# Block kernel with S5, block attention, retention and expert layer: decay rates on ScalarE, parameters loaded first, four blocks rounded by GpSimd, part of the second angles on ScalarE, key gains in tables and in a copy

## The chip, the cores and the metric

The kernel runs on one core of a Trainium2 chip. The metric is the device time of one execution in microseconds (us); lower is better. Three runs of the kernel before took 913.27, 913.45 and 913.71 us.

## The reference

One layer of a model with 256 tokens of width 1024 is computed. Its input projection feeds three mixers side by side; their outputs go through a second projection, and a layer of 16,384 experts follows.

```python
h = rms_norm(x, norm1_g)
ua, qb, kb, vb, qc, kc, vc, gc = split(h @ w_in)         # 256, 3 x 512, 4 x 256 columns
# S5 mixer on ua: 16 groups x 64 complex states
dt = exp(log_dt); mag = exp(lam_re * dt)                 # decay rates
ar = mag * cos(lam_im * dt); ai = mag * sin(lam_im * dt)
fr = ((ar - 1) * lr + ai * li) / (lr*lr + li*li); fi = (ai * lr - (ar - 1) * li) / (lr*lr + li*li)
bb = f * b; state[t] = a * state[t-1] + bb @ ua[t]; y = real(c @ state) + ua * d
ya = y' * sigmoid(y' @ w_glu), y' = gelu(y)
# block attention: rms_unit(q) * gq and rms_unit(k) * gk, the first 16 of 64 dims rotated; softmax
# retention: q, k rotated; decayed scores
y = concat(rms_unit(ya), rms_unit(yb), yc) * mix_out_g
x = x + y @ w_out
x = x + peer_layer(rms_norm(x, norm2_g))                 # 8 heads, top 16 of 128 x 128 experts
```

## The kernel before

**Products in halves.** A 32-bit operand is split into a high part, rounded to the format that TensorE multiplies at full rate, and a low part, the rest. Each product is three matmuls: high by high, high by low, low by high (lines 438 to 440). The projection weights (`w_in`, `w_out`, `w_q`) are cut into slices of 128 rows by 512 columns, numbered m = 0, 1, 2, ... in the order of use; slices 0 to 39 are `w_in`. A slice passes a line of four engines: a DMA on SyncE brings a group of eight slices (2 MB) into one of three places of `w_ring`; ScalarE rounds the slice into `w_hi` (`slices_high`, line 1387); GpSimd subtracts into `w_lo` (`slices_low`, line 1728); TensorE multiplies both token tiles, six matmuls of 512 columns (`by_slices`). `w_hi` and `w_lo` have four places each, so ScalarE may round slice m only once TensorE is done with slice m-4 (semaphore `half_used`). The order of every engine is written out by hand.

**The start.** x is transposed (line 415) and scaled by the norm gain into eight blocks `hT[:, k]`: blocks 0 to 3 by ScalarE (`full`, line 1426), 4 to 7 by VectorE (line 882). The first 256 columns of `w_in`, which give `ua`, are multiplied unsplit (line 455). ScalarE rounds the eight blocks into `h_hi` (`rounded`, line 1433) and GpSimd subtracts into `h_lo` (line 1759); slice k needs both. GpSimd alternates: blocks 0 to 3, slice 0, block 4, slice 1, and so on. Ahead of all this it computes `mag`, the exponential of `expo`, with a polynomial of small dependent instructions (lines 1736 to 1748).

**The S5 mixer in pieces.** VectorE derives `dt`, `expo` and the angles from the parameters `vec`, then the input matrices `bb`. The phases of the scan are a table of cosines and sines (`pc`, `pS`) in two halves of four tiles: `phase_turns` (VectorE, three passes of 1024 columns: product with time, add a rounding constant, take the fraction) then `phase_sines`, `phase_sizes`, `phase_cosines` (ScalarE). The drive of the states is multiplied in four parts by `drive(n)` on TensorE (line 430) between slices, and each part is scanned by `states(n)` on VectorE (lines 817 and 996). `drive(0)` stands after slice 2, `drive(1)` after slice 12. `states(0)` uses PSUM banks 6 and 7.

**Attention.** VectorE rotates queries (tables with the query gain in them) and keys. Each key tile is first multiplied by the gain (line 817, two instructions of 512 columns). TensorE transposes them (line 491) and ScalarE copies them out of PSUM (`heads_back`, line 1451). The negated output matrix `c_neg` (line 1081), in the place of `b_s`, is made by VectorE between `states(2)` and `states(3)`. The semaphore `consts_in` counts five loads (rotation table, `s5_c`, `w_glu`, `mask`, `decay`), 16 for each; VectorE first waits for all 80 behind `states(0)`.

**The rest.** From about 120 us on the second projection and the experts run in loops which the change leaves alone.

Of the kernel before, what the change touches and what calls it, by code (L numbers as in the profile page):

```python
# [57 lines left out]
POOL_HIGH = (34, 36)  # L58
TAIL = FRONT + 4 * KC
# [34 lines left out]
V_N = V_GQK + 2 * HD  # L94
# [28 lines left out]
def build(nc, x, w_in, vecs, consts, rots, decay, mask, s5_b, s5_c, w_glu, w_out, w_q, keys, u_t, v, out, spill):  # L123
    with ExitStack() as ctx:
# [84 lines left out]
        mask_s = rawf[:, 0:S]  # L209
        rope_q = rawf[:, 320:384].rearrange("p (f t d) -> p f t d", f=2, t=TT)  # L210
# [33 lines left out]
        turn_ready, phase_ready = sem("phase_turns_ready"), sem("phases_ready")  # L244
        bb_ready, bT_psum, bT_ready = sem("bb_ready"), sem("bT_in_psum"), sem("bT_ready")
# [18 lines left out]
        th_ready, tl_ready = sem("transposed_high_ready"), sem("transposed_low_ready")  # L264
        pq_ready, sc_psum, sc_ready = sem("pq_ready"), sem("keys_scores_in_psum"), sem("keys_scores_ready")
# [39 lines left out]
        phi_p = ps[:, 5, 0:8]  # L305
# [4 lines left out]
        spare = tiny(1)  # L310
        mag_k, mag_rest, mag_power = tiny(8), tiny(8), tiny(8)
# [96 lines left out]
        def _(pe):  # L408
# [51 lines left out]
            def by_slices(n, ks):  # L460

                for k in ks:
                    m = KC * (n - 1) + k
                    if n == 1:
                        pe.wait_ge(th_ready, k + 1)
# [183 lines left out]
            def out_slices(n, places):  # L649

                for i in places:
                    k = MIX_ORDER[i]
                    if n == 0:
                        pe.wait_ge(th_ready, KC + i + 1)
# [33 lines left out]
            for n in range(2):  # L688
                for k in range(KC):
                    if n == 0:  # L690
                        pe.wait_ge(th_ready, 2 * KC + k + 1)
# [29 lines left out]
            def keys_turn(t, groups=None, first=False, first_group=False, wide=()):  # L721

                for s in range(UN):
# [4 lines left out]
                    for h in range(2):  # L728
                        if first and s == 0:
                            pe.wait_ge(th_ready, 3 * KC + 4 * h + 4)  # L730
                            pe.wait_ge(tl_ready, 3 * KC + 4 * h + 4)
# [76 lines left out]
        def _(dve):  # L808
# [18 lines left out]
            V.memset(eps_4, 4 * EPS).then_inc(zeros_ready, 1)  # L827

            def transposed_low(gain, n, order=range(KC), banks=range(4), first=0):

                for i, k in enumerate(order, first):
                    dve.wait_ge(th_ready, n * KC + 2 * (i // 2) + 2)
# [23 lines left out]
            for part in (RC1, RC2, RC3):  # L856
# [13 lines left out]
            did(tt(cols(V_GQK + HD + ROPE, HD - ROPE), cols(V_GQK + HD + ROPE, HD - ROPE), cols(V_GQK + ROPE, HD - ROPE),  # L870
                   ALU.mult))
# [59 lines left out]
            tt(bb[:, 1], bb[:, 1], t_b, ALU.add).then_inc(bb_ready, 1)  # L931
            dve.wait_ge(bT_psum, 1)
            dve.wait_ge(u_ready, 1)
            did(V.tensor_copy(phi_p, phi))
# [89 lines left out]

            states(0)
            phase_turns(1, 6, phi_p)
# [18 lines left out]
            step(rotate([k_p[t][:, :, 0:ROPE] for t in range(TT)], k_p, half_rope, rope[:, 0], rope[:, 1], scratch(ROPE),  # L1045
# [35 lines left out]
            V.tensor_scalar(c_neg, c_s, -1.0, None, ALU.mult).then_inc(c_ready, 1)  # L1081
            dve.wait_ge(c_ready, 1)
# [96 lines left out]
            for k in range(KC + 2):  # L1179
                if k >= 2:  # L1180
                    dve.wait_ge(th_ready, 3 * KC + k - 1)
# [185 lines left out]
        def _(act):  # L1367
# [37 lines left out]

            def phase_sines(c):
# [22 lines left out]
            def rounded(ks):  # L1429

                for k in ks:
                    act.wait_ge(full_act if k < 4 else full_dve, k % 4 + 1)
# [16 lines left out]
            def heads_back(a, d_):  # L1449
                act.wait_ge(rotT_psum, a + 1)  # L1450
                A.activation(d_, ps[:, 6:8, :].rearrange("p b (h t) -> p (b h) t", h=2), ACT.Copy).then_inc(rotT_ready, 1)
# [15 lines left out]
            act.dma_start(vec[:], vecs).then_inc(params_in, 16)  # L1467
            act.dma_start(ident, consts[:, C_ID:C_ID + P]).then_inc(con_in, 16)
            act.dma_start(rawf[:, 256:256 + ROPE_N], rots[:, 0:ROPE_N]).then_inc(rope_in, 16)
            act.wait_ge(zeros_ready, 4)  # L1470
            A.activation(spare, quarter, ACT.Sqrt)
            squares_x(0)
            squares_x(1)
            act.wait_ge(params_in, 16)
            for k in range(4):
                full(k)
            act.wait_ge(sumsq_x, TT)
            root(ss_x, 0, 1.0 / D)
            rounded(range(0, 4))
# [4 lines left out]
            slices_high(range(0, 1))  # L1484
            rounded(range(4, KC))
# [3 lines left out]
            for t in range(TT):  # L1489
                A.activation(u_tok[:, t, :], ps[:, 4 + 3 * t, 0:S5_CH], ACT.Copy,  # L1490
                             scale=rx[:, t:t + 1]).then_inc(u_tok_ready, 1)
            slices_high(range(2, 3))
            act.wait_ge(uT_psum, 1)
            A.activation(uT, ps[:, 5, :].rearrange("p (c t) -> p c t", c=S5_C), ACT.Copy).then_inc(u_ready, 1)
            phase_sines(0)
            slices_high(range(3, 4))
            phase_sizes(0)
            slices_high(range(4, 5))
            phase_cosines(0)
            slices_high(range(5, 11))  # L1500
# [10 lines left out]
            heads_back(0, mqT)  # L1511
# [7 lines left out]
            heads_back(1, mkT)  # L1519
# [196 lines left out]
        def _(pool):  # L1716
# [14 lines left out]
            def step(ins):  # L1731
                did(ins)
                settle()

            pool.wait_ge(expo_ready, 1)
            step(G.tensor_scalar(mag_k, expo, float(1 / np.log(2)), ROUND, ALU.mult, ALU.add))
            step(G.tensor_scalar(mag_k, mag_k, -ROUND, None, ALU.add))
            step(G.tensor_scalar(mag_rest, mag_k, -LN2_1, None, ALU.mult))
            step(G.tensor_tensor(mag_rest, mag_rest, expo, ALU.add))
            step(G.tensor_scalar(mag_power, mag_k, -LN2_2, None, ALU.mult))  # L1740
            step(G.tensor_tensor(mag_rest, mag_rest, mag_power, ALU.add))
            step(G.tensor_scalar(mag_k, mag_k, -127.0, 127.0, ALU.max, ALU.min))
            step(G.tensor_scalar(mag_power.bitcast(mybir.dt.int32), mag_k, 127.0, float(2 ** 23), ALU.add, ALU.mult))
            step(G.tensor_scalar(mag, mag_rest, EXP_C[0], EXP_C[1], ALU.mult, ALU.add))
            for c_ in EXP_C[2:] + [1.0]:
                step(G.tensor_tensor(mag, mag, mag_rest, ALU.mult))
                step(G.tensor_scalar(mag, mag, c_, None, ALU.add))
            G.tensor_tensor(mag, mag, mag_power, ALU.mult).then_inc(mag_ready, 1)

# [7 lines left out]
            for k in range(KC):  # L1757
                pool.wait_ge(th_ready, k + 1)
# [41 lines left out]
def layout(inputs):  # L1800
# [4 lines left out]
    rep = lambda v_: np.broadcast_to(v_, (P, HD))  # L1805
    vecs = np.concatenate([
# [3 lines left out]
        rep(a["moba_q_g"]), rep(a["moba_k_g"])], axis=1)  # L1810
# [35 lines left out]
```

## Time and profile before

| | |
|---|---|
| median of 3 runs | 913.45 us |
| the profiled execution | 913.86 us |
| its span | 912.1 us |
| TensorE matmul busy | 899.2 us |
| VectorE, ScalarE, GpSimd busy | 725.6, 557.9, 432.4 us |
| HBM traffic | 173.86 MB read, 17.30 MB written |

The span runs from the first instruction to the last; 1.8 us of the execution lie around it. All times of the trace are counted from the start of the span. A matmul's shown length overlaps the next one's: matmuls of 512 columns follow each other every 0.23 us at the higher clock. PEclk is the share of full clock that was granted: 1.00 is 2.4 GHz and 0.50 is 1.2 GHz. In a row of the timeline, "x4" means that four instructions were merged: the second number is then the time from the start of the first to the end of the last.

### The profile page before, as it was taken

How to read it: one execution, taken by the hardware profiler on the slowest of the kernel's cores; microseconds unless marked ns; L12 is line 12 of the kernel's file. 1: busy time of each engine (PE TensorE's matmuls, PEld its weight loads, DVE VectorE, ACT ScalarE, POOL GpSimd, SP SyncE). 2: the span in 40 equal slices, each digit the busy share in tenths (PEclk: the TensorE clock that was granted, in tenths of full speed). 3: DMA queues.
4: the chain of work that ended last, by engine and by line, in shares of the span. 5: the costliest groups of instructions: out<-in, count | busy, mean ns of one | idle time of the engine just before them, and what ended most of it. 6: DMA issues, size and time to landing. Idle time of an engine off the chain costs nothing.

```text
span 912.1 us, 19216 instructions
## 1 busy us (share of the span) xinstructions
PE 899.2 (99%) x5348; PEld 792.0 (87%) x5348; DVE 725.6 (80%) x1635; ACT 557.9 (61%) x1123; POOL 432.4 (47%) x366
## 2 busy tenths in 40 slices
PE   6999999999999999999999999999999999999998
PEld 5777889899999999999999999888888888888886
DVE  6799634199998339999999996888888888888886
ACT  5668556655555566666666666565666656656663
POOL 5876278888888987777777774000000000000000
PEclk9999999999999999999999999999999999999999
DMA  9553150466666675565556557767777777776773
GB/s 338 206 185 115 72 204 5 162 225 219 231 228 227 230 229 188 194 219 197 193 185 215 199 180 241 247 237 246 243 243 240 233 246 245 241 242 233 242 248 129
DMA packets 67756, 191.54 MB, mean 210 GB/s; under 512 B 6672, under 2 KB 8592, under 8 KB 67728
## 3 DMA queue, kind: packets, MB, share of 16 engines
q1 hardware_dynamic: 67296, 191.00, 61.4%
q8 instruction: 15, 0.25, 0.1%
q10 hardware_dynamic: 432, 0.19, 0.1%
q14 instruction: 13, 0.11, 0.0%
HBM read 173.86 MB, written 17.30 MB: 210 GB/s over the span
## 4 chain that ended last, share of the span: by engine, by line
PE 94%; DVE 3%; POOL 1%; DMA 0%; issue 0%; ACT 0%; DVEq 0%
PE ps L438 23%; PE ps L440 23%; PE ps L439 23%; PE ps L744 13%; PE ps L746 6%; PE ps L754 3%; PE ps L743 1%; DVE routing L817 1%; DVE ps L817 1%; DVE ps L996 1%; DMA vec<-in_vecs 0%; PE ps L717 0%; PE ps L595 0%; PE ps L430 0%; POOL h_both L1759 0%
## 5 line engine op out<-in xcount | busy, mean ns | idle before, releaser
L1601 ACT ACTIVATE w_hi<-raw 128x512 fp32r<-128x512 f32 x512 | 308.3, 628 | 130.6 <-PE ps L440 126.9
L1773 POOL TENSOR_TENSOR w_lo<-raw,w_hi 128x512 fp32r<-128x512 f32 x256 | 327.4, 1300 | 72.5 <-ACT w_hi L1601 72.1
L817 DVE TENSOR_TENSOR w_lo<-raw,w_hi 128x512 fp32r<-128x512 f32 x256 | 177.4, 693 | 51.1 <-ACT w_hi L1601 40.1
L438 PE MATMUL ps<-w_hi,hot_gate 128*128 128x512 f32 x512 | 199.2, 389 | 0.0
L439 PE MATMUL ps<-w_lo,hot_gate 128*128 128x512 f32 x512 | 199.2, 389 | 0.0
L440 PE MATMUL ps<-w_hi,hot_gate 128*128 128x512 f32 x512 | 199.2, 389 | 0.0
L744 PE MATMUL ps<-h_both,w_hi 128*128 128x512 f32 x504 | 181.3, 397 | 0.0
L438 PE MATMUL ps<-h_both,w_hi 128*128 128x256 f32 x584 | 165.6, 284 | 0.0
L440 PE MATMUL ps<-h_both,w_lo 128*128 128x256 f32 x584 | 165.2, 283 | 0.0
L439 PE MATMUL ps<-h_both,w_hi 128*128 128x256 f32 x584 | 165.2, 283 | 0.0
L746 PE MATMUL ps<-h_both,w_lo 128*128 128x256 f32 x441 | 123.8, 281 | 0.0
L440 PEld LDWEIGHTS ps<-w_hi,hot_gate 128*128 128x128 f32 x512 | 96.1, 188 | 20.0
L439 PEld LDWEIGHTS ps<-w_lo,hot_gate 128*128 128x128 f32 x512 | 96.1, 188 | 20.0
L438 PEld LDWEIGHTS ps<-w_hi,hot_gate 128*128 128x128 f32 x512 | 96.1, 188 | 19.8
L438 PEld LDWEIGHTS ps<-h_both,w_hi 128*128 128x128 f32 x584 | 111.8, 192 | 0.4 <-POOL w_lo L1728 0.2
L439 PEld LDWEIGHTS ps<-h_both,w_hi 128*128 128x128 f32 x584 | 111.9, 192 | 0.1
L440 PEld LDWEIGHTS ps<-h_both,w_lo 128*128 128x128 f32 x584 | 111.9, 192 | 0.0
L1728 POOL TENSOR_TENSOR w_lo<-routing,w_hi 128x512 fp32r<-128x512 f32 x72 | 92.0, 1301 | 41.6 <-ACT w_hi L1387 40.8
L744 PEld LDWEIGHTS ps<-h_both,w_hi 128*128 128x128 f32 x504 | 94.3, 188 | 17.2
L1303 DVE SCALAR_TENSOR_TENSOR hot_gate<-ps,route_t 128x256 fp32r<-128x256 f32 x256 | 105.7, 476 | 0.0
L1630 ACT ACTIVATE acts<-ps 128x256 f32<-128x256 f32 x128 | 49.2, 384 | 92.0 <-PE ps L440 81.4
L817 DVE TENSOR_TENSOR route_t<-acts,routing 128x256 f32<-128x256 f32 x128 | 81.6, 638 | 6.3 <-DMA acts<-act_spill 3.2
(243 smaller groups left out, 1164.3 us busy)
## 6 DMA issues: line engine op xcount, KB each, us to landing
raw<-in_u_t SPq DMA_DIRECT2D x128, 512.0 KB, 3.5
raw<-in_v SPq DMA_DIRECT2D x128, 512.0 KB, 3.4
act_spill<-acts SPq DMA_DIRECT2D x62, 256.0 KB, 2.2
acts<-act_spill SPq DMA_DIRECT2D x62, 256.0 KB, 3.4
routing<-in_w_in SPq DMA_DIRECT2D x4, 2048.0 KB, 11.6
routing<-in_w_out SPq DMA_DIRECT2D x2, 2048.0 KB, 8.2
routing<-in_w_q SPq DMA_DIRECT2D x2, 2048.0 KB, 7.9
routing<-in_w_in SPq DMA_DIRECT2D x2, 1024.0 KB, 10.2
```

The source lines that it names most:

```text
L438: pe.matmul(dst, s_hi, m_hi, start=first and i == 0, stop=False)
L439: pe.matmul(dst, s_hi, m_lo, start=False, stop=False)
L440: mm = pe.matmul(dst, s_lo, m_hi, start=False, stop=end)
L744: mm = pe.matmul(ps[:, s % 2, :], s_hi, both, start=(h == 0 and k == 0), stop=end)
L746: mm = pe.matmul(ps[:, s % 2, 0:S], s_lo, m_hi, start=False, stop=False)
L754: mm = pe.matmul(ps[:, 4 + 2 * (s % 2) + q // 2, (q % 2) * 2 * NKEY:(q % 2 + 1) * 2 * NKEY], hot_j[:, s % 2, q, :], hot_gate[:, s % 2, q]. ...
L817: return V.tensor_tensor(out_, a, b, op)
L1303: ins = V.scalar_tensor_tensor(hot_gate[:, s % 2, q], iota_p.unsqueeze(1).to_broadcast([P, 2, NKEY]), route_t[:, 0, one], route_t[:, 2:4, ...
L1601: A.activation(w_hi[:, 2 * (s % 2) + h, :], raw[:, s, h * HALF:(h + 1) * HALF], ACT.Copy)\
L1630: A.activation(acts[:, s, :], ps[:, s % 2, 0:S], ACT.Gelu_apprx_tanh).then_inc(act_ready, 1)
L1728: G.tensor_tensor(w_lo[:, m % 4, :], w_ring[n % W_SLOTS][:, k, :], w_hi[:, m % 4, :].bitcast(F32), ALU.subtract).then_inc(lo_ready, 1)
L1773: G.tensor_tensor(w_lo[:, slot, :], raw[:, s, h * HALF:(h + 1) * HALF], w_hi[:, slot, :].bitcast(F32), ALU.subtract).then_inc(lo_ready, 1)
```

## The change

1. `mag` is one ScalarE instruction (Exp), placed between the two squares of x; GpSimd's polynomial is gone. The early ScalarE instruction that loaded the Sqrt table is gone too.
2. The load of `vec` is SyncE's first DMA; it was ScalarE's first.
3. Blocks 4 to 7 are rounded by GpSimd (a cast), each just ahead of its subtraction. ScalarE rounds blocks 0 to 3 and slice 0, then computes the root for `rx`.
4. `phase_turns(0)` comes ahead of `rx` on VectorE; ScalarE's three steps for the first phases move a place or so forward.
5. The second half of the turns: `second_turns` on ScalarE computes the product with time (four copies with a scale, into PSUM banks 6 and 7) and adds the rounding constant; it stands between slices 9 and 10 and waits for `states(0)`, which uses the same banks. VectorE keeps the last pass.
6. The key gain: its rotated dims go into a table of their own (`rope_k`, three small VectorE instructions), the others as a scale into ScalarE's copy of the transposed keys. The two multiplications of 512 columns are gone; the query's own gain for the other dims is in the same factor.
7. `c_neg` and its wait for `consts_in` come ahead of `states(0)`.

The core of the diff:

```diff
         def _(sp):
+            sp.dma_start(vec[:], vecs).then_inc(params_in, 16)
             for t in range(TT):
                 sp.dma_start(xs[:, t, :], x[t * P:(t + 1) * P, :]).then_inc(x_in[t], 16)
...
+            phase_turns(0, 2, phi)
             rstd_of(1, 0, TT, rx[:, 0:TT]).then_inc(rx_ready, 1)
-            phase_turns(0, 2, phi)
...
-            did(V.tensor_copy(phi_p, phi))
...
+            dve.wait_ge(consts_in, 80)
+            V.tensor_scalar(c_neg, c_s, -1.0, None, ALU.mult).then_inc(c_ready, 1)
+            dve.wait_ge(c_ready, 1)
             states(0)
-            phase_turns(1, 6, phi_p)
+            dve.wait_ge(rounded_up, 1)
+            V.scalar_tensor_tensor(pair(zb[:, 4:8]), pair(xr[:, 4:8]), -ROUND,
+                                   ps[:, 6:8, :].rearrange("p b (j t) -> p b j t", j=2), ALU.add,
+                                   ALU.subtract).then_inc(turn_ready, 1)
...
-            for t in range(TT):
-                did(tt(k_p[t], k_p[t], cols(V_GQK + HD, HD).unsqueeze(1).to_broadcast([P, MH, HD]), ALU.mult))
-            settle()
...
             states(2)
-            V.tensor_scalar(c_neg, c_s, -1.0, None, ALU.mult).then_inc(c_ready, 1)
-            dve.wait_ge(c_ready, 1)
             states(3)
...
+            def second_turns():
+
+                act.wait_ge(states_ready, 1)
+                turns = ps[:, 6:8, :].rearrange("p b (j t) -> p (b j) t", j=2)
+                for j in range(4):
+                    did(A.activation(turns[:, j], times, ACT.Copy, scale=phi[:, 4 + j:5 + j]))
+                settle()
+                A.activation(xr[:, 4:8], turns, ACT.Identity, bias=round_up).then_inc(rounded_up, 1)
...
             squares_x(0)
+            act.wait_ge(expo_ready, 1)
+            A.activation(mag, expo, ACT.Exp).then_inc(mag_ready, 1)
             squares_x(1)
...
-            slices_high(range(5, 11))
+            slices_high(range(5, 10))
+            second_turns()
+            slices_high(range(10, 11))
             projected(0)
...
             for k in range(KC):
-                pool.wait_ge(th_ready, k + 1)
+                if k < 4:
+                    pool.wait_ge(th_ready, k + 1)
+                else:
+                    pool.wait_ge(full_dve, k - 3)
+                    G.tensor_copy(h_hi[:, k, :], hT[:, k, :]).then_inc(th_pool, 1)
+                    pool.wait_ge(th_pool, k - 3)
```

ScalarE around slice 10 (`w_hi<-routing` is the rounding of a slice) before, from slice 8 on:

```order
L1387 ACTIVATE w_hi<-routing 128x512 [waits half_used,weights_in2]
L1387 ACTIVATE w_hi<-routing 128x512 [waits half_used] x2
L1440 ACTIVATE routing<-ps,small 128x512 [waits half_used]
L1440 ACTIVATE routing<-ps,small 128x512
L1387 ACTIVATE w_hi<-routing 128x512 [waits half_used]
L1447 ACTIVATE routing<-routing 128x1024 [waits proj_ready]
```

and now:

```order
L1398 ACTIVATE w_hi<-routing 128x512 [waits half_used,weights_in2]
L1398 ACTIVATE w_hi<-routing 128x512 [waits half_used]
L1422 ACTIVATE ps<-con,small 128x256 [waits states_ready]
L1422 ACTIVATE ps<-con,small 128x256 x3
L1424 ACTIVATE routing<-ps,small 128x1024 [waits act_steps]
L1398 ACTIVATE w_hi<-routing 128x512 [waits half_used]
L1460 ACTIVATE routing<-ps,small 128x512 [waits half_used]
L1460 ACTIVATE routing<-ps,small 128x512
L1398 ACTIVATE w_hi<-routing 128x512 [waits half_used]
L1467 ACTIVATE routing<-routing 128x1024 [waits proj_ready]
```

Five instructions stand between the roundings of slices 9 and 10, the first with a wait for VectorE's `states_ready`. VectorE from the end of the input matrices `bb` to the start of `states(0)` now (the third row of the piece before was a copy of `phi`):

```order
L821 TENSOR_TENSOR raw<-raw,vec 128x32
L821 TENSOR_TENSOR raw<-raw,vec 128x2x8 x2
L944 COPY raw<-ps 128x512 [waits u_ready,bT_in_psum,dve_steps]
L1035 TENSOR_SCALAR raw<-raw 128x512 [waits consts_in]
L821 TENSOR_TENSOR route_t<-ps,routing 128x512 [waits bu_in_psum,phases_ready,c_negated]
L821 TENSOR_TENSOR route_t<-ps,routing 128x512
```

The negation (line 1035) and its wait for `consts_in` now stand ahead of the first instruction of `states(0)`. GpSimd at the start now:

```order
L1767 TENSOR_TENSOR h_both<-routing,h_both 128x256 [waits transposed_high_ready] x4
L1750 TENSOR_TENSOR w_lo<-routing,w_hi 128x512 [waits hi_ready]
L1765 CAST h_both<-routing 128x256 [waits h_full_by_dve]
L1767 TENSOR_TENSOR h_both<-routing,h_both 128x256 [waits transposed_high_by_pool]
L1750 TENSOR_TENSOR w_lo<-routing,w_hi 128x512 [waits hi_ready]
L1765 CAST h_both<-routing 128x256 [waits h_full_by_dve]
```

The polynomial ahead of the first row is gone, and a cast stands ahead of each of the subtractions of blocks 4 to 7.

## Rows read from the trace of the kernel before

**Rows 1.** The page: busy time of each engine, share, instructions.

```profile
PE 899.2 (99%) x5348; PEld 792.0 (87%) x5348; DVE 725.6 (80%) x1635; ACT 557.9 (61%) x1123; POOL 432.4 (47%) x366
```

**Rows 2.** TensorE by stretches: from:to, us, busy (matmuls), PEclk, DMA share, GB/s.

```profile
16.00:18.00 2.00, 0.00 (x0) 1.00 1.04 384
18.00:20.00 2.00, 0.00 (x0) 0.61 1.05 388
25.00:26.00 1.00, 1.00 (x5) 0.87 1.05 389
```

**Rows 3.** Timeline, TensorE: start, us, line, operation, idle before and releaser.

```profile
8.48 7.14 PE L455 MATMUL ps<-routing 128*128 128x256 f32 x32
20.66 0.77 PE L438 MATMUL ps<-w_hi,h_both 128*128 128x512 f32 x1 [5.03 <-POOL w_lo L1728]
30.56 0.40 PE L438 MATMUL ps<-w_hi,h_both 128*128 128x512 f32 x1
38.74 0.39 PE L438 MATMUL ps<-w_hi,h_both 128*128 128x512 f32 x1
42.92 1.13 PE L430 MATMUL ps<-routing,raw 32*128 32x256 f32 x8
```

**Rows 4.** Timeline, parameters, GpSimd and ScalarE at the start.

```profile
8.20 0.20 POOL L1736 TENSOR_SCALAR small<-small 128x8 f32<-128x8 f32 x1 [7.77 <-DVE small L817]
16.52 2.77 POOL L1759 TENSOR_TENSOR h_both<-routing,h_both 128x256 fp32r<-128x256 f32 x4
19.25 1.26 POOL L1728 TENSOR_TENSOR w_lo<-routing,w_hi 128x512 fp32r<-128x512 f32 x1
4.89 0.17 DVE L839 TENSOR_SCALAR small<-vec 128x8 f32<-128x8 f32 x1 [3.88 <-DMA vec<-in_vecs]
7.87 1.57 ACT L1426 ACTIVATE routing<-ps,vec 128x256 f32<-128x256 f32 x4 [0.52 <-PE ps L415]
10.85 1.28 ACT L1481 ACT_TABLE_LOAD   x1
```

**Rows 5.** DMA issues, 0 to 4 and 12 to 16 us: KB each, us to landing.

```profile
routing<-in_w_in SPq DMA_DIRECT2D x1, 1024.0 KB, 9.1
acts<-in_decay SPq DMA_DIRECT2D x1, 512.0 KB, 10.3
```

**Rows 6.** Timeline, SyncE's queue: the issues of these two loads.

```profile
3.35 0.45 SPq L346 DMA_DIRECT2D routing<-in_w_in  x1
15.11 0.63 SPq L355 DMA_DIRECT2D acts<-in_decay  x1
```

**Rows 7.** Timeline, VectorE: first and last row of states(0), then `c_neg`.

```profile
29.26 1.29 DVE L817 TENSOR_TENSOR route_t<-ps,routing 128x512 f32<-128x512 f32 x2 [1.78 <-PE ps L430]
35.85 2.61 DVE L817 TENSOR_TENSOR routing<-ps,routing 128x512 f32<-128x512 f32 x4
84.81 0.43 DVE L1081 TENSOR_SCALAR raw<-raw 128x512 f32<-128x512 f32 x1
```

**Rows 8.** Timeline, ScalarE: rounding of slices 10 to 12 and what stands between.

```profile
34.86 0.63 ACT L1387 ACTIVATE w_hi<-routing 128x512 fp32r<-128x512 f32 x1 [0.73 <-PE ps L440]
36.23 1.27 ACT L1440 ACTIVATE routing<-ps,small 128x512 f32<-128x512 f32 x2 [0.73 <-PE ps L440]
37.38 0.63 ACT L1387 ACTIVATE w_hi<-routing 128x512 fp32r<-128x512 f32 x1
37.90 1.06 ACT L1447 ACTIVATE routing<-routing 128x1024 f32<-128x1024 f32 x1
38.85 1.15 ACT L1387 ACTIVATE w_hi<-routing 128x512 fp32r<-128x512 f32 x2
```

**Rows 9.** Timeline, GpSimd: subtraction of slice 11.

```profile
38.09 1.31 POOL L1728 TENSOR_TENSOR w_lo<-routing,w_hi 128x512 fp32r<-128x512 f32 x1 [0.75 <-ACT w_hi L1387]
```

**Rows 10.** GpSimd's cast of a slice (line 1755): duration in ns, min, median, max.

```profile
L1755 POOL CAST w_hi<-routing x2: 613/616/618, 75.9 to 79.3; 128x512 fp32r<-128x512 f32 x2
```

**Rows 11.** Waits of TensorE from 28 to 165 us.

```profile
PE ps L595 <- DVE routing L817: 0.9, 1, 0.9
```

More of the change, by code:

```diff
@@ L58 @@
 POOL_HIGH = (34, 36)
+TH0 = 4
 TAIL = FRONT + 4 * KC
@@ L93 @@
 V_GQK = 50
-V_N = V_GQK + 2 * HD
+V_HEAD = V_GQK + 2 * HD
+V_N = V_HEAD + 2
 C_ID, C_IOTA = 0, P
@@ L209, in build @@
         mask_s = rawf[:, 0:S]
+        rope_k = rawf[:, 384:448].rearrange("p (f t d) -> p f t d", f=2, t=TT)
         rope_q = rawf[:, 320:384].rearrange("p (f t d) -> p f t d", f=2, t=TT)
@@ L244, in build @@
         turn_ready, phase_ready = sem("phase_turns_ready"), sem("phases_ready")
+        rounded_up = sem("second_turns_rounded")
         bb_ready, bT_psum, bT_ready = sem("bb_ready"), sem("bT_in_psum"), sem("bT_ready")
@@ L264, in build @@
         th_ready, tl_ready = sem("transposed_high_ready"), sem("transposed_low_ready")
+        th_pool = sem("transposed_high_by_pool")
         pq_ready, sc_psum, sc_ready = sem("pq_ready"), sem("keys_scores_in_psum"), sem("keys_scores_ready")
@@ L309, in build @@
         std = tiny(32)
-        spare = tiny(1)
-        mag_k, mag_rest, mag_power = tiny(8), tiny(8), tiny(8)
+        spare, round_up = tiny(1), tiny(1)
         hmax, hsum = tiny(16), tiny(16)
@@ L464, in by_slices @@
                     if n == 1:
-                        pe.wait_ge(th_ready, k + 1)
+                        pe.wait_ge(th_ready, min(k + 1, 4))
                         pe.wait_ge(tl_ready, k + 1)
@@ L653, in out_slices @@
                     if n == 0:
-                        pe.wait_ge(th_ready, KC + i + 1)
+                        pe.wait_ge(th_ready, TH0 + i + 1)
                         pe.wait_ge(tl_ready, KC + i + 1)
@@ L690, in _ @@
                     if n == 0:
-                        pe.wait_ge(th_ready, 2 * KC + k + 1)
+                        pe.wait_ge(th_ready, TH0 + KC + k + 1)
                         pe.wait_ge(tl_ready, 2 * KC + k + 1)
@@ L729, in keys_turn @@
                         if first and s == 0:
-                            pe.wait_ge(th_ready, 3 * KC + 4 * h + 4)
+                            pe.wait_ge(th_ready, TH0 + 2 * KC + 4 * h + 4)
                             pe.wait_ge(tl_ready, 3 * KC + 4 * h + 4)
@@ L827, in _ @@
             V.memset(eps_4, 4 * EPS).then_inc(zeros_ready, 1)
+            V.memset(round_up, ROUND).then_inc(zeros_ready, 1)
             def transposed_low(gain, n, order=range(KC), banks=range(4), first=0):
                 for i, k in enumerate(order, first):
-                    dve.wait_ge(th_ready, n * KC + 2 * (i // 2) + 2)
+                    dve.wait_ge(th_ready, TH0 + (n - 1) * KC + 2 * (i // 2) + 2)
                     place = H2_PLACE[k] if n == 2 else k
@@ L931, in _ @@
             tt(bb[:, 1], bb[:, 1], t_b, ALU.add).then_inc(bb_ready, 1)
+            g_k = V_GQK + HD
+            did(tt(rope_k[:, 0], rope[:, 0], cols(g_k, ROPE).unsqueeze(1).to_broadcast([P, TT, ROPE]), ALU.mult))
+            for a, b in ((0, half_rope), (half_rope, 0)):
+                did(tt(rope_k[:, 1, :, a:a + half_rope], rope[:, 1, :, a:a + half_rope],
+                       cols(g_k + b, half_rope).unsqueeze(1).to_broadcast([P, TT, half_rope]), ALU.mult))
+            settle()
             dve.wait_ge(bT_psum, 1)
             dve.wait_ge(u_ready, 1)
-            did(V.tensor_copy(phi_p, phi))
             V.tensor_copy(bT, ps[:, 6, :].rearrange("p (a s) -> p a s", a=4)).then_inc(bT_ready, 1)
@@ L1041, in _ @@
             k_p = psum_heads(6)
-            for t in range(TT):
-                did(tt(k_p[t], k_p[t], cols(V_GQK + HD, HD).unsqueeze(1).to_broadcast([P, MH, HD]), ALU.mult))
-            settle()
-            step(rotate([k_p[t][:, :, 0:ROPE] for t in range(TT)], k_p, half_rope, rope[:, 0], rope[:, 1], scratch(ROPE),
+            step(rotate([k_p[t][:, :, 0:ROPE] for t in range(TT)], k_p, half_rope, rope_k[:, 0], rope_k[:, 1], scratch(ROPE),
                         (1.0, 1.0)))
@@ L1180, in _ @@
                 if k >= 2:
[L1181 removed]
+                    dve.wait_ge(th_ready, TH0 + 2 * KC + k - 1)
                     tt(h_lo[:, H2_PLACE[k - 2], :], ps[:, 1 + (k - 2) % 3, 0:S], h_hi[:, H2_PLACE[k - 2], :].bitcast(F32),
@@ L1431, in rounded @@
                 for k in ks:
-                    act.wait_ge(full_act if k < 4 else full_dve, k % 4 + 1)
+                    act.wait_ge(full_act, k + 1)
                     A.activation(h_hi[:, k, :], hT[:, k, :], ACT.Copy).then_inc(th_ready, 1)
@@ L1447, in square_heads, with heads_back @@
                 A.activation(mv, dst[n], ACT.Square).then_inc(qk_sq, 1)
-            def heads_back(a, d_):
+            def heads_back(a, d_, gain):
                 act.wait_ge(rotT_psum, a + 1)
-                A.activation(d_, ps[:, 6:8, :].rearrange("p b (h t) -> p (b h) t", h=2), ACT.Copy).then_inc(rotT_ready, 1)
+                A.activation(d_, ps[:, 6:8, :].rearrange("p b (h t) -> p (b h) t", h=2), ACT.Copy,
+                             scale=gain).then_inc(rotT_ready, 1)
             def exps(places):
@@ L1476, in _ @@
                 full(k)
+            rounded(range(0, 4))
+            slices_high(range(0, 1))
+            act.wait_ge(zeros_ready, 5)
             act.wait_ge(sumsq_x, TT)
             root(ss_x, 0, 1.0 / D)
-            rounded(range(0, 4))
             act.wait_ge(ang_ready, 1)
@@ L1483, in _ @@
             A.activation(c1, half, ACT.Sin).then_inc(trig_ready, 1)
-            slices_high(range(0, 1))
-            rounded(range(4, KC))
             slices_high(range(1, 2))
@@ L1491, in _ @@
                              scale=rx[:, t:t + 1]).then_inc(u_tok_ready, 1)
+            phase_sines(0)
             slices_high(range(2, 3))
@@ L1494, in _ @@
             A.activation(uT, ps[:, 5, :].rearrange("p (c t) -> p c t", c=S5_C), ACT.Copy).then_inc(u_ready, 1)
-            phase_sines(0)
+            phase_sizes(0)
             slices_high(range(3, 4))
-            phase_sizes(0)
+            phase_cosines(0)
             slices_high(range(4, 5))
-            phase_cosines(0)
-            slices_high(range(5, 11))
+            slices_high(range(5, 10))
+            second_turns()
+            slices_high(range(10, 11))
             projected(0)
@@ L1510, in _ @@
             slices_high(range(17, 20))
-            heads_back(0, mqT)
+            heads_back(0, mqT, 1.0)
             act.wait_ge(rotT_ready, 1)
@@ L1518, in _ @@
             slices_high(range(24, 28))
-            heads_back(1, mkT)
+            heads_back(1, mkT, cols(V_HEAD, 1))
             slices_high(range(28, 33))
@@ L1729, in slices_low @@
                                     w_hi[:, m % 4, :].bitcast(F32), ALU.subtract).then_inc(lo_ready, 1)
[L1731 to L1748, printed above, removed]
             def slice_high(m):
@@ L1805, in layout @@
     rep = lambda v_: np.broadcast_to(v_, (P, HD))
+    ones = np.ones(ROPE, f)
+    down = lambda v_: np.concatenate([ones, v_[ROPE:], ones, v_[ROPE:]])[:, None]
     vecs = np.concatenate([
@@ L1809, in layout @@
         per(np.repeat(a["s5_log_dt"], S5_STATE), S5_T), per(a["s5_d"], S5_C),
-        rep(a["moba_q_g"]), rep(a["moba_k_g"])], axis=1)
+        rep(a["moba_q_g"]), rep(a["moba_k_g"]), down(a["moba_q_g"]), down(a["moba_k_g"])], axis=1)
     b = np.zeros((P, 2, S5_T, 32), f)
```

11 lines of the change are left out of this document (4 added, 7 removed).

## The prediction

> **What bounds the kernel now.** The page comes first: TensorE is busy for 899.2 of 912.1 us [rows 1], so work taken off other engines counts only where TensorE waits for it. The waits of TensorE come next. From 28 us on there is one of 0.9 us, for VectorE in front of line 595 [rows 11], and little else. The large one is at the start: after the unsplit projection, which ends at 8.48 + 7.14 = 15.62, TensorE idles 5.03 us for GpSimd's first `w_lo` [rows 3]. GpSimd had spent 8.20 to 16.52 on the polynomial for `mag` [rows 4]. The windows add a second price: the granted clock fell from 1.00 to 0.50 between 18 and 20 us, after some three idle microseconds, and rose again between 25 and 26 (0.87, so at about 25.26) [rows 2]. From 20.66 that is 4.6 us at 1.2 instead of 2.4 GHz, a loss of 2.3 us of matmul work. The question is how much of these 7 us comes back, and whether the new order keeps TensorE fed from there to `drive(1)` at 42.92.
>
> **The start, step by step.** The parameters land before 4.89 [rows 4]. As SyncE's first load they have no x ahead of them; I take 3.2, an estimate between the issue at 0.7 and that 4.9 (no gain); the sum below turns out not to depend on it. VectorE's chain to `expo`, 3.3 us long (4.89 to 8.20, where GpSimd was released [rows 4]), then ends at 6.5. The Exp on ScalarE waits for that and delays the second square by about 0.5 us, but the transposes' copies start about 7.87 [rows 4] in any case, so I cost that at 0.2 (at the late bound it is 2). The rounding of blocks 0 to 3 ends near 11.0. Slice 0 then waits for its weights, which land at 3.35 + 9.1 = 12.45 [rows 5, 6], and is rounded at 13.1. Behind it stand two table loads of 1.28 [rows 4] with the root between them, so the sines are done near 16.4 and slice 1 at 17.0. VectorE has `bb` some 3.8 us after the sines, at 20.3, as early as before.
>
> GpSimd starts on `h_lo` near 10.0: four times 0.69 (2.77/4), then slice 0 until 14.5 [rows 4]. TensorE ends the projection at 15.7 and goes straight on, at full clock. For blocks 4 to 7 GpSimd needs per slice a cast, which I take as 0.35, a bit more than half of the 0.616 for 512 columns [rows 10], plus 0.7 and 1.26 [rows 4], some 2.5 us with the semaphores. Above, a cast could cost as much as a whole 512-column one (0.62, in all 1.1 us more); below, the bare half (0.31). Chaining this with `bb`, slice 2 is multiplied from 21.0, `drive(0)` from 22.4 to 23.5, and slice 4 at 26.2, where it was 30.56 [rows 3]: 4.35 us ahead. Slice 9 would be done at about 34.4. Weights don't hold this up: ScalarE's rows for slices 10 to 12 had waited for TensorE or for nothing [rows 8].
>
> **The wait that takes its place.** Slice 10 now depends on a chain through three engines:
> - `c_neg` and all of `states(0)` behind it wait for the five loads counted by `consts_in`. The last one, `decay`, lands at 15.11 + 10.3 = 25.4 [rows 5, 6]. The DMA engines are saturated all that time (share 1.04 to 1.05, 384 to 389 GB/s [rows 2]), and the change moves no bytes in or out of that queue but the 0.09 MB of parameters, so I keep 25.4; 24.9 and 25.9 are the bounds.
> - `c_neg` costs 0.43 and the wait behind it 0.03, as at 84.81 [rows 7]: 25.86. In the kernel before, `states(0)` needed nothing but `drive(0)`.
> - `states(0)` takes 35.85 + 2.61 - 29.26 = 9.20 us [rows 7]: done at 35.06.
> - `second_turns` on ScalarE waits for it, and queued behind it are slice 10 and everything after. Its four copies I take from the four of line 1426, also 256 columns with a scale: 1.57. The 1024-column addition I take from the square of the same size: 1.06 [rows 4, 8]. No row has exactly these forms with PSUM as target; 2.2 to 3.2 us are my bounds. Slice 10 is taken up at 37.7.
> - Rounding 0.63 [rows 8], hand-over 0.08 and subtraction 1.31 [rows 9], hand-over 0.15: TensorE starts slice 10 at 39.85, against 38.74 before [rows 3].
>
> So TensorE stands still from 34.4 to 39.85, the 4.35 us of the start are used up, and 1.1 us more. The same wait would stand there if `drive(0)` came two microseconds sooner or later: the loads set it. That makes this term firm and the details of the start indifferent.
>
> Slices 11 and 12 need their own chain: from slice 10's rounding, 0.52 to `projected(0)`, 1.15 to slice 11, 0.52 to the squares, 0.95 to slice 12 (37.38, 37.90, 38.85 [rows 8]). Slice 12 is rounded from 40.8, GpSimd delivers it at 42.8, and `drive(1)` starts at 44.4 even at full clock: 1.5 us late.
>
> **The clock.** An idle time of 5.4 us is longer than the one of 5.03 us after which the clock had fallen [rows 2, 3]. I expect it at 1.2 GHz again when slice 10 starts. The row's price is 2.3 us for 4.6 us at the lower level; below stands nothing, if it rises at once. I take 1.6, nearer to the row since the idle time is the like. Then slices 10 to 12, 4.18 us at full clock (42.92 - 38.74 [rows 3]), are done at 39.85 + 4.18 + 1.6 = 45.6, and they, not ScalarE, are what is late. `drive(1)` starts 2.7 us later than before; with 2.3 it would be 3.4.
>
> The Trainium skill (TensorE: Matmul & The Clock Gate, "Part 1: The HAM clock gate") says that the monitor's sampling runs free of the program, so that a kernel spends a varying time cold from run to run. By that rule the term may come out anywhere from about nothing to more than the row's 2.3, and the sum between 914.5 and 917. The trace agrees as to the two levels, 1.00 and 0.50; no repeated fall in it could show the variation.
>
> **What VectorE saves.** One pass for the product with time and one for the constant (the 1024-column passes, some 2.5 us), the copy of `phi` and the two key multiplications (1.3 us) go. Behind `drive(1)` TensorE's matmuls release VectorE each time, and TensorE waits only once, at line 595 [rows 11]. The stretch in front of that wait contains `c_neg`: 0.43 + 0.03 [rows 7] come back there. The others lie ahead of TensorE's own scores, and hide behind its matmuls: 0. If they bore on that wait too, all 0.9 us of it could go; nothing more.
>
> **Sum.** +1.1 for slice 10, +1.6 for its clock, -0.5 for line 595: +2.2 us. The profiled execution took 913.86, so 916.1 in its terms; it stands 0.4 above the median of the three runs, 913.45, and I forecast 915.7 for the median. Everything behind `drive(1)` is TensorE-bound and shifts as a whole.
>
> **Rivals.**
> - *The clock does not fall, or rises at once.* For it: the idle time could be shorter, if the start gains less than I think. Against: the like idle time made it fall. Then the 1.5 us of the supply count: 913.45 + 1.5 - 0.5 = 914.5.
> - *The loads don't hold `states(0)`.* If `decay` lands by 23.5, `states(0)` starts with the drive at 23.6, slice 10 comes at 37.6, 1.1 ahead of before, and 0.4 of that goes for slices 11 and 12: 912.3 at full clock, 914 with the slow one. Against: the landing at 25.4 and a saturated queue.
> - *The start's gain comes through: faster.* This needs slice 10 supplied as the queue runs, without the wait for `states_ready` in between. The point is TensorE's end of slice 9 at 34.4: if slice 10 is rounded by 33.0, nothing is lost, and the gain is 4.35 + 0.46 = 4.8 us: 908.7. For it: ScalarE is only 61% busy [rows 1], and 4.35 us of lead are large. Against: 9.20 us of `states(0)` stand between `drive(0)` and it, whatever else moves. The Trainium skill (GPSIMD Engine Reference, "Performance versus the Vector engine") says GpSimd is about twice as slow as VectorE at elementwise work; by that price the four casts would take about twice their 0.35, and this rival would give 1.4 less, 910.1. Here the trace disagrees: the cast of 512 columns took 0.616 us, no more than ScalarE's 0.63 [rows 8, 10].
> - *The change does not bring the parameters early.* Then the start gains 2 us less, and the wait for slice 10 swallows the difference: 915.7 still, or 914.5 with a shorter idle time.
>
> **How the numbers follow.** The forecast has a chance of 0.64, with its own range of 914.6 to 917.2. A clock that stays up has 0.13, loads that don't hold `states(0)` 0.13, the gain that comes through 0.10. Two runs of this kernel can be told apart at about 0.2%, or 1.8 us: below 911.6 is faster, above 915.3 slower. Of the 0.64 three quarters lie above 915.3, which is 0.48 for slower. The rest of it and the two middle cases are no change: 0.42. Faster is 0.10. The range, 912.4 to 917.2, leaves out the last rival and the far end of a long slow clock.
>
> **What would show it.** Right: VectorE idle up to about 25.4 in front of line 1035, `states(0)` from 25.9 to 35.1; ScalarE idle behind slice 9 for `states_ready`; GpSimd idle for ScalarE before slice 10; TensorE without the gap at 15.6 but with one of about 5 us ending at 39.9, and a granted clock of 0.50 there; line 595's wait down to 0.4. Wrong: slice 10 multiplied at 34 to 37, or `drive(1)` before 43, or `c_neg` run before 24.

## The result

The changed kernel takes 917.90 us (median of 5 runs, 917.35 to 920.05), the kernel before 913.45 (5 runs, 913.27 to 914.03). The ratio is 1.0049 with a 95% interval of 1.0032 to 1.0067: slower, by 4.45 us. The forecast was 915.7, with 917.2 as the upper end of the range. The direction and the place were right; the forecast rise of 2.25 us was half of what came.

The profiled execution took 917.35 us, its span is 915.5, so 3.4 us more than the span before. TensorE's large waits come first. This is the timeline of TensorE, only the rows that answer to [rows 3]:

```profile
9.04 7.76 PE L459 MATMUL ps<-routing 128*128 128x256 f32 x32
...
16.45 0.58 PE L442 MATMUL ps<-w_hi,h_both 128*128 128x512 f32 x1
...
26.56 0.47 PE L442 MATMUL ps<-w_hi,h_both 128*128 128x512 f32 x1 [0.52 <-POOL w_lo L1750]
...
40.70 0.79 PE L442 MATMUL ps<-w_hi,h_both 128*128 128x512 f32 x1 [5.62 <-POOL w_lo L1750]
...
46.77 1.13 PE L434 MATMUL ps<-routing,raw 32*128 32x256 f32 x8
```

The gap of 5.03 us at the start is gone: the first slice starts at 16.45, 0.4 us before the shown end of the projection (9.04 + 7.76). Slice 4 starts at 26.56, 4.0 us ahead of 30.56. Then a gap of 5.62 us stands in front of slice 10, which starts at 40.70, 1.96 us later than before, and `drive(1)` starts at 46.77, 3.85 us later. Behind it nothing changes but line 599 (595 before), which waited 0.9 us [rows 11]. All waits of TensorE matmuls from 28 to 165 us (total, times, longest):

```profile
PE ps L442 <- POOL w_lo L1750: 5.6, 1, 5.6
PE ps L599 <- DVE routing L821: 0.4, 1, 0.4
PE ps L442 <- issue: 0.3, 1, 0.3
PE ps L649 <- DVE routing L821: 0.2, 1, 0.2
```

3.85 - 0.5 = 3.35, which is the 3.4 of the spans. The chain behind the gap, in VectorE's timeline (answers to [rows 7]):

```profile
25.58 1.12 DVE L1035 TENSOR_SCALAR raw<-raw 128x512 f32<-128x512 f32 x1 [2.79 <-DMA acts<-in_decay]
26.73 1.29 DVE L821 TENSOR_TENSOR route_t<-ps,routing 128x512 f32<-128x512 f32 x2
...
33.32 2.61 DVE L821 TENSOR_TENSOR routing<-ps,routing 128x512 f32<-128x512 f32 x4
```

then ScalarE's (answers to [rows 8]) and GpSimd's subtraction of slice 10 (to [rows 9]):

```profile
35.97 1.67 ACT L1422 ACTIVATE ps<-con,small 128x256 f32<-128x256 f32 x4 [5.68 <-DVE routing L821]
37.67 1.11 ACT L1424 ACTIVATE routing<-ps,small 128x1024 f32<-128x1024 f32 x1
38.68 0.62 ACT L1398 ACTIVATE w_hi<-routing 128x512 fp32r<-128x512 f32 x1
39.20 1.26 ACT L1460 ACTIVATE routing<-ps,small 128x512 f32<-128x512 f32 x2
...
39.37 1.27 POOL L1750 TENSOR_TENSOR w_lo<-routing,w_hi 128x512 fp32r<-128x512 f32 x1 [6.53 <-ACT w_hi L1398]
```

VectorE waits 2.79 us and is released by the load of `decay`, ScalarE waits 5.68 us for VectorE, GpSimd 6.53 us for ScalarE, TensorE 5.62 us for GpSimd: a delay handed through four engines. The load makes only the first part of it. In e1 below, `states(0)` begins 1.25 us after the start of `drive(0)`; here that would be at 24.57. The load holds it until 25.58 (1.0 us), then `c_neg` until 26.73 (1.15 us), and the 9.20 us of `states(0)` itself follow. The windows of TensorE (from:to, us, busy, PEclk, DMA share, GB/s; answers to [rows 2]) show the second price:

```profile
34.00:36.00 2.00, 1.08 (x5) 1.00 1.05 407
36.00:38.00 2.00, 0.00 (x0) 0.93 0.70 263
38.00:40.00 2.00, 0.00 (x0) 0.50 0.03 10
40.00:42.00 2.00, 1.30 (x3) 0.50 0.00 0
42.00:44.00 2.00, 2.00 (x6) 0.50 0.00 0
44.00:46.00 2.00, 2.00 (x10) 0.86 0.00 0
```

The granted clock fell to 0.50 near 37.7, after 2.6 idle microseconds, and was back near 44.6. Slices 10 to 12 took 46.77 - 40.70 = 6.07 us where they had taken 4.18.

### The profile page after: what moved, and what is told of

It is laid out like the page before. It is cut to its first block, busy times and chain, and to the rows that moved or that the text cites. A ratio compares the mean times of both kernels' runs of the same rounds, so it can differ in the third digit from the quotient of the medians.

```text
span 915.5 us, 19198 instructions
## 1 busy us (share of the span) xinstructions
PE 902.4 (99%) x5348; PEld 793.3 (87%) x5348; DVE 723.5 (79%) x1634; ACT 560.4 (61%) x1125; POOL 428.3 (47%) x346
## 4 chain that ended last, share of the span: by engine, by line
PE 92%; DVE 4%; SPq 2%; DMA 1%; ACT 1%; issue 0%; POOL 0%; DVEq 0%
PE ps L442 22%; PE ps L444 22%; PE ps L443 22%; PE ps L748 13%; PE ps L750 6%; PE ps L758 3%; DMA acts<-in_decay 1%; DVE routing L821 1%; DVE ps L821 1%; PE ps L747 1%; DVE ps L1005 1%; SPq L355 1%; PE ps L721 0%; DVE route_t L821 0%; PE ps L599 0%; DVE xs L821 0%
```

## Experiments

Theory 1: slice 10 comes a fixed chain after the later of `drive(0)` and the loads (c_neg, states(0), second turns, rounding, subtraction), and the idle time it makes costs a second time by the clock. The rivals: ScalarE's added work as such; supply or DMA; a start that gained nothing. All times below are medians, with the ratio to the kernel before of the same batch and its 95% interval.

**e1: `c_neg` behind `states(0)`.**

```diff
-            dve.wait_ge(consts_in, 80)
-            V.tensor_scalar(c_neg, c_s, -1.0, None, ALU.mult).then_inc(c_ready, 1)
-            dve.wait_ge(c_ready, 1)
             states(0)
+            dve.wait_ge(consts_in, 80)
+            V.tensor_scalar(c_neg, c_s, -1.0, None, ALU.mult).then_inc(c_ready, 1)
+            dve.wait_ge(c_ready, 1)
```

> The changed kernel with c_neg and its wait for the five loads put behind states(0), ahead of the last pass of the second turns. Theory 1 (the loads hold states(0), and by it slice 10): states(0) starts when drive(0) ends, near 24.5 instead of 26.73 us, slice 10 at 38.5 instead of 40.70, and the time falls by 2.2 us to 915.7. GpSimd has nothing to do at the new place, so c_neg should be back at 0.43 us if GpSimd was what made it 1.12. Rival (ScalarE's five extra instructions alone make the gap, the loads don't matter): 917.9 as before, slice 10 near 40.7. If the clock no longer falls for a gap that is 2.2 us shorter, 914 or less.

915.35 us, ratio 1.0021 (1.0012 to 1.0030). That is 2.6 us less than the change. VectorE and TensorE:

```profile
24.73 1.29 DVE L821 TENSOR_TENSOR route_t<-ps,routing 128x512 f32<-128x512 f32 x2 [1.77 <-PE ps L434]
...
33.95 0.43 DVE L1036 TENSOR_SCALAR raw<-raw 128x512 f32<-128x512 f32 x1
```

```profile
38.69 0.80 PE L442 MATMUL ps<-w_hi,h_both 128*128 128x512 f32 x1 [3.54 <-POOL w_lo L1750]
44.51 1.13 PE L434 MATMUL ps<-routing,raw 32*128 32x256 f32 x8
```

`states(0)` starts with the drive, and slice 10 2.0 us sooner. The edit takes two things out of the chain at once, the wait for the loads (1.0 us) and `c_neg` itself (1.15 us with its wait), and together they cost this much, and no more: the gap is still 3.5 us, and the clock fell again in it, so that slice 10 to `drive(1)` took 5.82 us. The remainder is the wait for `states(0)` itself.

**e2: TensorE kept busy in the gap.**

```diff
-            by_slices(2, range(0, 5))
+            by_slices(2, range(0, 2))
+            keep_warm(ident, 5, 20)
+            by_slices(2, range(2, 5))
```

> The changed kernel with 20 small matmuls of the identity with itself, results unused, on TensorE between slices 9 and 10, in the gap of 5.6 us; nothing else moves. Theory 1 (the clock's fall costs the time of slices 10 to 12, and its rise at a varying moment makes the runs spread): granted clock 1.00 throughout, slice 10 still near 40.7, drive(1) near 45.2 instead of 46.77, time 1.5 to 2 us lower, about 916.1, and the runs within 0.5 us of each other. Rival (the slow slices and the spread have another cause, such as supply or the DMA): 917.9 and a spread of 1 us or more as before.

918.17 us, ratio 1.0050 (1.0036 to 1.0063): the expected 916.1 was missed. The 20 matmuls (the trace shows two records for each) filled 4.63 us, but `decay` landed 0.6 us later in this execution, and an idle time of 2.48 us was left, in which the clock fell again:

```profile
40.00:42.00 2.00, 0.43 (x1) 0.76 0.00 0
42.00:44.00 2.00, 2.00 (x6) 0.50 0.00 0
44.00:46.00 2.00, 2.00 (x10) 0.88 0.00 0
```

So this run does not test the clock's term. A hint is that the one run of the five with a mean granted clock of 1.000 took 916.19, and the others, at 0.996 to 0.998, took 917.69 to 918.93.

**e5: the same with 27.**

```diff
-            keep_warm(ident, 5, 20)
+            keep_warm(ident, 5, 27)
```

> As e2 with 27 small matmuls instead of 20, so that they last until slice 10 is supplied; in e2 an idle 2.5 us was left and the clock fell all the same. Theory 1 (the fall of the clock is a term of its own, some 2 us): granted clock 1.00 at slice 10, slices 10 to 12 in 4.2 to 4.5 us instead of 6.07, drive(1) near 45.3, and 915.5 to 916.3, like the one run of e2 whose clock stayed at 1.000 (916.19). Rival (the clock is no term): 917.9 to 918.2.

916.45 us, ratio 1.0032 (1.0021 to 1.0043), at a clock of 1.000 in five of seven runs. All seven lie within 0.8 us, the change's five within 2.7. The profile shows slice 10 at full speed:

```profile
35.76 6.19 PE L427 MATMUL ps<-con 128*128 128x128 f32 x54
41.70 0.48 PE L442 MATMUL ps<-w_hi,h_both 128*128 128x512 f32 x1
42.02 0.40 PE L443 MATMUL ps<-w_lo,h_both 128*128 128x512 f32 x1
...
46.32 0.92 PE L434 MATMUL ps<-routing,raw 32*128 32x256 f32 x6
```

From slice 10 to `drive(1)` it is 4.62 us instead of 6.07, with the granted clock at 1.00 throughout. That is what shows the clock to be a term of its own, worth 1.45 us here; the whole line runs about 0.9 us later in this execution (`c_neg` had to wait until 26.45 for its load), and so the spans differ by only 0.5. The medians differ by 1.45 us too, but they come from two batches and their intervals just overlap. Work that computes nothing also brought the runs closer together. That the clock makes most of the spread is not shown: the two e5 runs at 0.998 and 0.999 took 916.48 and 916.43, no more than the others, and the change's five runs do not sort by their mean clock.

**e3: all three passes of the second turns on VectorE**, `c_neg` behind them.

```diff
-            second_turns()
...
             states(0)
-            dve.wait_ge(rounded_up, 1)
-            V.scalar_tensor_tensor(pair(zb[:, 4:8]), pair(xr[:, 4:8]), -ROUND, ...
+            phase_turns(1, 6, phi_p)
+            dve.wait_ge(consts_in, 80)
+            V.tensor_scalar(c_neg, c_s, -1.0, None, ALU.mult).then_inc(c_ready, 1)
```

> The changed kernel with the second turns back on VectorE, all three passes, and c_neg behind them; no ScalarE work stands between slices 9 and 10. Theory 1 (the start's gain is real and is lost in the gap before slice 10): slice 4 at 26.6 as in the changed kernel, drive(1) at 39.0, 3.9 us ahead of the kernel before, line 599 half a microsecond less: 909.1. Rival (something else than second_turns takes the start's gain, such as the supply of slices 4 to 12 by a later GpSimd or weights that come too late): 911 to 914.

909.69 us, ratio 0.9961 (0.9950 to 0.9973): 3.7 us faster than the kernel before and 8.2 faster than the change. TensorE has no wait at slice 10:

```profile
23.22 1.13 PE L435 MATMUL ps<-routing,raw 32*128 32x256 f32 x8
...
26.46 0.47 PE L443 MATMUL ps<-w_hi,h_both 128*128 128x512 f32 x1 [0.53 <-POOL w_lo L1747]
...
38.92 1.13 PE L435 MATMUL ps<-routing,raw 32*128 32x256 f32 x8
```

The start's 4.0 us are real and come through whole once nothing stands between slices 9 and 10 (this run moves `c_neg` as well).

**e4: the second turns on ScalarE, three slices later** (on top of e1).

```diff
             slices_high(range(5, 10))
-            second_turns()
             slices_high(range(10, 11))
             projected(0)
             slices_high(range(11, 12))
             square_heads(0)
-            slices_high(range(12, 15))
+            slices_high(range(12, 13))
+            second_turns()
+            slices_high(range(13, 15))
```

> As e1, and second_turns stands behind the rounding of slice 12 instead of slice 9 on ScalarE. By then states(0) is over (near 33.7 us), so ScalarE should not wait for it. Theory 1 (the place of the wait, not the work of 2.7 us, was the harm): no gap before slice 10, drive(1) at 39.0 to 39.3, 909.0 to 909.5. Rival (2.7 us of work on ScalarE are too much anywhere in front of drive(1)): TensorE waits 1 to 2 us for slice 13 or for the turns, 910.5 to 912.

910.18 us, ratio 0.9969 (0.9957 to 0.9981). The gap before slice 10 is gone with the same work still on ScalarE: its place was the harm. In between the two expectations, since a small wait came up at `drive(1)`, for VectorE's last pass:

```profile
39.27 1.13 PE L434 MATMUL ps<-routing,raw 32*128 32x256 f32 x8 [0.58 <-DVE routing L1040]
```

**e7: that wait put behind `drive(1)`** (on top of e4).

```diff
-            pe.wait_ge(turn_ready, S5_C)
             drive(1)
             by_slices(2, range(5, KC))
+            pe.wait_ge(turn_ready, S5_C)
             turn_heads(0)
```

> As e4, and TensorE's wait for the second turns stands ahead of the transposes of the queries instead of ahead of drive(1), which uses other banks. In e4 it waited 0.6 us there. Theory 1: that wait goes and nothing takes its place, 0.6 us below e4: 909.3. Rival (the DVE is then late with states(1) or the queries, and TensorE waits later): 909.9 as e4.

909.70 us, ratio 0.9959 (0.9945 to 0.9972). From slice 4 to `drive(1)` it takes 12.43 us in this profile (27.18 to 39.61) against 13.08 in e4's (26.19 to 39.27), so the wait is gone in the trace; in the medians the 0.5 us are inside the intervals. Slice 4 came 1.0 us later beside loads that landed later: TensorE waited 1.81 us for x at 7.87, and ScalarE could take up slice 0 at 13.96 only, where e4 has 12.98. e3 and e7 cannot be told apart.

**e6: the two waits alone**, on the kernel before: `second_turns` between slices 9 and 10, and `c_neg` ahead of `states(0)`.

```diff
+            dve.wait_ge(consts_in, 80)
+            V.tensor_scalar(c_neg, c_s, -1.0, None, ALU.mult).then_inc(c_ready, 1)
+            dve.wait_ge(c_ready, 1)
             states(0)
-            phase_turns(1, 6, phi_p)
+            dve.wait_ge(rounded_up, 1)
+            V.scalar_tensor_tensor(pair(zb[:, 4:8]), pair(xr[:, 4:8]), -ROUND, ...
...
-            slices_high(range(5, 11))
+            slices_high(range(5, 10))
+            second_turns()
+            slices_high(range(10, 11))
```

> The kernel before with two parts of the change alone: second_turns on ScalarE between slices 9 and 10, and c_neg with its wait ahead of states(0). The start is as before, so drive(0) ends at 29.1, after the loads (25.6). Theory 1 (slice 10 comes a fixed chain of 9.2 + 2.8 + 2.2 us after the later of drive(0) and the loads): c_neg hides, states(0) runs 29.3 to 38.5, slice 10 at 43.4 against 38.74, a gap of 4.6 us, slow clock behind it: 918.5 to 919.5, more than the whole change. Rival (as the prediction put it, the start doesn't matter since the loads set slice 10): 917.9.

919.96 us, ratio 1.0067 (1.0051 to 1.0082): worse than the whole change, and above the expected 918.5 to 919.5. Slice 10 comes at 42.82 after a gap of 4.49 us, `drive(1)` at 49.35:

```profile
42.82 0.80 PE L439 MATMUL ps<-w_hi,h_both 128*128 128x512 f32 x1 [4.49 <-POOL w_lo L1745]
49.35 1.13 PE L431 MATMUL ps<-routing,raw 32*128 32x256 f32 x8
```

The start does matter: it brings `states(0)` from 28.86 here to 26.73 in the change, the 2.1 us by which slice 10 differs. Only what it gained beyond the loads is lost. One part of the theory needs a correction: what released `states(0)` here was neither `drive(0)` nor the loads but ScalarE's last step for the first phases. What stands is the fixed chain behind it. From the start of `states(0)` to slice 10 it took 13.96 or 13.97 us in the change, e1, e2 and e6, and 14.10 in e5, whose extra matmuls ran until slice 10 came.

**e8: e3 with GpSimd's polynomial back.**

```diff
-            act.wait_ge(expo_ready, 1)
-            A.activation(mag, expo, ACT.Exp).then_inc(mag_ready, 1)
...
+            pool.wait_ge(expo_ready, 1)
+            step(G.tensor_scalar(mag_k, expo, float(1 / np.log(2)), ROUND, ALU.mult, ALU.add))
+            ...
```

> As e3, with the decay rates on GpSimd's polynomial again. Theory 1 (GpSimd's polynomial was most of the start's loss): GpSimd begins it at 6.3 when expo is there, ends near 14.6, slice 0 is delivered at 18.8 instead of 15.3, TensorE waits 2.4 us at 16.4, with the clock staying up after so short an idle time; 2 to 2.5 us more than e3: 911.9. Rival (the early parameters and the table order made the gain): 910.

911.15 us, ratio 0.9974 (0.9964 to 0.9984): 1.2 us above e3 by the ratios, half of what I expected. The first slice comes at 18.82, 3.2 us later than in e3, after an idle time of 3.36 us, and the clock, which I had expected to stay up, fell (0.52 from 20 to 22 us). Yet `drive(1)` is only 1.96 us later than in e3 (40.88). The likely reason is that the first slices are paced by GpSimd's cast and two subtractions, so that TensorE's lateness is partly covered. The polynomial was some 1.2 to 1.7 us of the start's gain (the spans are 909.6 and 907.9); the rest belongs to the earlier parameters and casts, which I have not separated.

## Why the prediction was right in kind and wrong in size

Two terms of the sum were too small, `c_neg` (0.43 taken, 1.12 measured) and the clock (1.6 taken, 1.9 measured), and the step from the profiled execution to the median added another 1.0 us. The rest of the chain held.

*The start.* Right within 1 us. Slice 4 was put at 26.2 and came at 26.56; `drive(0)` was put at 22.4 and came at 23.32. `vec` had landed by 2.96; 3.2 was taken. The cast took 0.40 us (0.35 taken):

```profile
L1765 POOL CAST h_both<-routing x4: 394/398/399, 15.3 to 24.0; 128x256 fp32r<-128x256 f32 x4
```

*The loads set `states(0)`.* Right as to the landing: 25.58 against 25.4. Since `drive(0)` came 0.9 us later than put, the load itself held `states(0)` for 1.0 us only; the 2.6 us that e1 won are this, `c_neg`, and what followed from both.

*`c_neg` costs 0.43.* This step failed: 1.12. I took the duration at 84.81, where GpSimd was idle (its subtractions stand at 80.81 to 84.60 and from 85.68). At 25.58 GpSimd was busy without a pause. It took 0.43 us where GpSimd was idle (the kernel before, e1), and 1.12 (the change), 1.35 (e2), 1.03 (e3), 1.11 (e5), 1.29 (e6) and 0.72 (e8) where it worked. In e4 and e7 it began some 0.15 us before a subtraction ended and took 0.44 and 0.43. The load on the DMA engines is not what differs: their share was 1.03 beside e1's 0.43 us and 0.00 beside e3's 1.03. The rows of e6, VectorE's first:

```profile
26.62 1.29 DVE L1027 TENSOR_SCALAR raw<-raw 128x512 f32<-128x512 f32 x1
26.34 1.29 POOL L1745 TENSOR_TENSOR w_lo<-routing,w_hi 128x512 fp32r<-128x512 f32 x1 [1.19 <-ACT w_hi L1393]
27.59 0.91 POOL L1776 TENSOR_TENSOR h_both<-routing,h_both 128x256 fp32r<-128x256 f32 x1
```

`c_neg` ends at 27.91, 0.32 us after GpSimd has gone on to its next instruction, and that one takes 0.91 us instead of 0.74. In the other five it is the same: `c_neg` ends 0.32 to 0.34 us after the start of GpSimd's next subtraction (26.37 in the change, 27.24 in e2, 38.06 in e3, 27.24 in e5, 40.02 in e8), and this takes 1.47 to 1.49 us instead of 1.28. So the price is no fixed factor. In these six executions it is the rest of the instruction that GpSimd is busy with when `c_neg` begins. The Trainium skill (GPSIMD Engine Reference, "1. Specifications") lists GpSimd's memory interfaces as shared with VectorE, with contention for VectorE instructions in a two-port mode or with two SBUF inputs. The traces agree that there is contention; in which mode `c_neg` ran none of them shows. The bounds of the prediction held no such case.

*The second turns, rounding, hand-overs.* Right: from 35.97 to 38.68 it is 2.71 us, 2.63 was taken; slice 10 at 40.70 instead of 39.85, of which 0.69 are `c_neg` and 0.18 the load.

*The clock.* The mechanism was right, the term too small: 1.6 was taken, the profile shows 6.07 - 4.18 = 1.9. The same difference is 1.6 in e1, 1.5 in e2 and 2.35 in e6, so the row's 2.3 was one draw among several, and so is this 1.9. A mean granted clock of 0.996 over the span, as here and in the profile before, stands for some 7 us at half speed. But it does not say where: e1's 0.996 is made of two falls, one at the start (0.50 from 8 to 11 us, after an idle time of 1.67 us) and one before slice 10. In the kernel before, the 35 runs of the experiments' batches go by the mean clock: 911.78 to 911.98 in the six runs at 1.000, 913.06 to 913.43 in the ten at 0.998, 913.32 to 914.72 in the 17 at 0.996 (single runs at 0.997 and 0.999 took 915.24 and 913.93). The three times that I had lay within 0.44 us and hid this.

*VectorE's savings.* Right in size: 0.5 us at line 599, nothing elsewhere. That it is `c_neg` that gave them, as I argued, two runs support together: the wait is 0.4 in e6, which keeps the two key multiplications, and in e3, which keeps all three passes of the second turns on VectorE; `c_neg` has moved in both.

*Sum.* `drive(1)` was put 2.7 us late and is 3.85: +0.85 for slice 10 (`c_neg`, load), +0.3 for the clock. This makes 3.35 in place of 2.2 in the profile, and the profiled executions differ by 3.49. With these two terms right I would have forecast about 916.85, which is still inside the range. The last 1.0 us of the miss comes from the step from the profile to the median: I carried the 0.4 by which the profiled execution before lies above its median over to the new kernel, whose profiled execution is the fastest of its five and lies 0.55 below. Two of the other four have a lower mean clock (0.994, 917.65 and 918.29), but 920.05 has 0.995 and 917.90 has 0.996, so the clock does not order them. What moves them, the 920.05 above all, is open.

*The claim that the start's details are indifferent* held for what they gained beyond the landing of the loads and was too broad: in e6, with the old start, slice 10 came 2.1 us later still.

*Rivals.* The clock that stays up was e5's case (916.45), not the change's. Loads that do not hold `states(0)` were e1 (915.35; I gave 912.3 to 914). The clock's price there was the 1.6 that I took; what was wrong is the start of `states(0)`, 24.73 instead of 23.6, and with it slice 10, 38.69 instead of 37.6. The gain that comes through was e3 and e7: 909.7 against 908.7.

## What to carry to other kernels

Before work is moved onto an engine that feeds another in order, ask what that work waits for, not only how long it takes: 2.7 us on ScalarE were nearly free behind slice 12 and cost 5.2 us behind slice 9 (e4 against e1). A semaphore that counts several loads puts the last of them in front of whatever waits, here a 512 KB load that nobody needed yet. A price from a row holds for what its neighbours did there. Look up what GpSimd does at the new place before taking over the price of a VectorE instruction of this kind: here it was 0.43 us, plus up to the rest of GpSimd's current instruction. And a profile is one execution: how far it lies from the median of its own kernel says nothing about the next one.

## Hardware that I had not expected

- A one-input VectorE instruction of 512 columns from SBUF to SBUF took 0.43 us beside an idle GpSimd and 0.72 to 1.35 us beside a busy one. It ended 0.32 to 0.34 us after GpSimd's current instruction had given way to the next, in six executions of six. Four two-input instructions with one input in PSUM took 2.61 us beside an idle GpSimd (the change at 33.32) and 2.61 beside a busy one (the kernel before at 82.16).
- TensorE's clock fell around idle times of 5.6 us (the change), 3.5 (e1) and 2.5 (e2), and at the start even of 1.67 (e1) and 1.81 (e7). 27 matmuls that compute nothing, 54 records in the trace, kept it up and won 1.45 us between slice 10 and `drive(1)`.
- The same program's executions lie up to 3.5 us apart (the kernel before, 911.78 to 915.24 in 35 runs). The mean clock sorts most of these. It does not sort those of e8, which lie within 0.3 us at 0.998 to 1.000, though the clock fell at the start of its profiled execution: a sign that a fall costs little where TensorE is not what the rest waits for. In e3 and e7, where no long idle time is left in the line, the clock stayed at 1.000 in eight of twelve runs.
